# Opening a projection phase with two weight slabs at once

## The chip, the cores and the metric

One core of a Trainium2 chip runs the kernel. The metric is the device time of one execution in microseconds; the profile is of one such execution. Engines are named as the profile does: PE is TensorE (matmuls), DVE VectorE, ACT ScalarE, POOL GpSimd, SP the engine that issues most DMAs.

## The reference

One inference step of a two-layer encoder for 544 tokens (512 of a prompt, 32 of a sample), model width 1024, all in fp32:

```
layer 0: h = rmsnorm(x); u,v,z,xbc,dt = h @ W_in
         x += concat(gmlp(u, v), rmsnorm(ssd(xbc, dt) * silu(z))) @ W_out
layer 1: h = rmsnorm(x); q,k,v,g = h @ W_in      (8 retention heads)
         x += (silu(g) * head_norm(retention(q, k, v))) @ W_out
each:    h = rmsnorm(x); x += (silu(conv3(h @ W_gate)) * (h @ W_up)) @ W_down
         x += sigmoid(rmsnorm(x) @ W_pgate) * (p @ W_pproj)
end:     y = rmsnorm(x)
```

Here rmsnorm(x) is x times the reciprocal root of the mean of its squares over the 1024 features, times a gain per feature.

## The kernel before

**Layout.** Features lie on the 128 partitions and the 544 tokens along the free dimension, so x is eight tiles of 128x544. An operand of a projection is held twice, as `op_hi` (rounded to the matmul's format) and `op_lo` (the rest), eight tiles each. Weights come in slabs: one slab (128 x 1024) holds the eight 128x128 blocks that give one output tile. A slab is loaded to `w_raw` and split into `w_hi` by ACT (`split_high`, L340) and `w_lo` by POOL (`split_low`, L414). There are four slots (RING = 4), and slab s+4 is split when slab s has been multiplied.

**A slab on PE** (`slab`, matmul at L318). For each operand tile k it makes three passes (w_hi x op_hi, w_hi x op_lo, w_lo x op_hi), each in two halves of the tokens: 6 matmuls a tile, 48 a slab. It signals `tile_done` at the end. The output `proj` has room for two slabs; a slab waits until DVE has evicted the output of the one before the last (`tile_read`). Slabs are grouped in phases, run in the order written in `phase_table`.

**Norms.** The scale 1/rms of a token is applied at the eviction of the outputs, not to the operand, so a phase can start before its norm is known. While the phase ahead ends, each finished tile of x goes through: ACT writes op_hi (`act_operand`, L376) and the square (L384), DVE writes op_lo (`dve_operand`, L389), POOL adds the square to `ssq` (`pool_square`, L405). After the last tile PE sums `ssq` over partitions with two matmuls against ones (`mean_square`, L329 and L330), ACT takes the root (`act_root`, L363 and L364), DVE the reciprocal (`dve_rstd`, L369). Only then can the first slab of the phase be evicted (`scaled`, L1393 and L1396, reads `rstd`).

**The openings.** Four phases have operands that carry a norm so computed: `outb` (norm n_yb), `gu00` (n_ffn0), `heads_a` (n_mix1) and `gu10` (n_ffn1). In each, PE runs slab 0, waiting for every tile's op_lo by the argument `ready`, then `mean_square`, then slab 1, slab 2 and so on. Phases gate0 and gate1 also carry a norm, but their `mean_square` stands between pp and gate.

**Order on the other engines.** Each engine's order is written out by hand. ACT and POOL run `phase(name, job)`: for each slab n first the split of slab n+4 (`split_ahead`, which waits for `tile_done` of slab n; `low_ahead`), then the job. In the gate phases ACT's job is the sigmoid of the evicted tile, and then op_hi and the square of the updated x; POOL's job adds the square. DVE between them multiplies the gate by `p_proj` (L1753) and adds to x (L1755). In gate1 the slabs from the fifth on have no slab s+4, so nothing is split there.

In a gate-up phase (gu) even slabs are the gate branch: DVE evicts, copies two columns of conv state (L1697), makes three taps (L1707, L1709), ACT makes SiLU, POOL multiplies by `rstd` (L604), and only then DVE evicts the odd slab (L1717, L1718).

Of the kernel before, what the change touches and what calls it, by code (L numbers as in the profile page):

```python
# [115 lines left out]
def build(nc, A, O):  # L116
# [27 lines left out]
    with ctx:  # L144
# [197 lines left out]
        def split_ahead(act, ph, n):  # L342

            s = n + ph.s0
            if not n.k and s.c + RING >= NSLABS:
                return
            g = (n * ph.m) + (ph.g0 + ph.m)
            act.wait_ge(tile_done, g.v)
            split_high(act, s + RING)
# [67 lines left out]
        def low_ahead(pool, ph, n):  # L417
            s = n + (ph.s0 + RING)
            if n.k or s.c < NSLABS:
                split_low(pool, s)  # L420
# [6 lines left out]
        HID = (1, 0)  # L427
        U_FIRST = 4
        WARM = 8
        V_SCALED = {1: (0, 1, 2), 3: (3, 4, 5), 4: (6, 7)}  # L430
        SSD_PIECES = ((1, 1, 5, 2, 2),) * NC + ((1, 1, 5, 2, 3),)
        SSD_MIXED = ((), (2,), (3,), (5,), (6,))
# [98 lines left out]
        @block.gpsimd  # L531
        def _(pool):
            sub, mul = ALU.subtract, ALU.mult

            def phase(name, job=None, per=4):
                def one(n):
                    low_ahead(pool, PH[name], n)
                    if job:
                        job(n)
                each_ahead(pool, PH[name], one, per)  # L540

            pool_squares(pool, "n_in", None)
            for n in range(RING):
                split_low(pool, At(n))
            pool.wait_ge(sem("wdt_hi"), 1)
            nc.gpsimd.tensor_tensor(w_dt_lo[:, :], w_dt[:, :], w_dt_hi[:, :], sub).then_inc(sem("wdt_lo"), 1)
            phase("v")

            phase("u")
            phase("xbc")  # L550
            low_ahead(pool, PH["outa"], At(0))

            def chunk(p, rows):

                pool.wait_ge(sem("x_copied"), 3 * p + 3)
                if p:
                    pool.wait_ge(sem("y_turned"), 2 * p)
                c = NC if p == 0 else p - 1
                three = lambda b, n: b[0:rows, 0:n * SP_].rearrange("p (h q) -> p h q", h=n)
                nc.gpsimd.tensor_tensor(three(y_tok, SH), three(x_tok, SH),  # L560
                                        head_rows[0:rows, 2 * SH:3 * SH].unsqueeze(2).broadcast_to([rows, SH, SP_]),
                                        mul).then_inc(sem("y_skip"), 1)
                pool.wait_ge(sem("xs_done"), p + 1)
                if p:
                    pool.wait_ge(sem("st_mm"), 2 * p)
                nc.gpsimd.tensor_tensor(three(xsd, SH), three(xs, SH),
                                        dte[0:rows, c * SH:(c + 1) * SH].unsqueeze(2).broadcast_to([rows, SH, SP_]),
                                        mul).then_inc(sem("xsd_done"), 1)

            for p in range(NC + 1):  # L570
                chunk(p, TS if p == 0 else CH)
                for n in SSD_MIXED[p] + SSD_END[p]:
                    low_ahead(pool, PH["outa"], At(n))
            pool_squares(pool, "n_yb", "n_in")
            phase("z", lambda n: pool_square(pool, "n_yb", n))
            pool_squares(pool, "n_ffn0", "n_yb")
            phase("outb", lambda n: pool_square(pool, "n_ffn0", n))

            for layer in range(2):
                if layer:  # L580
                    def head(name, h, h0):

                        for r_ in range(6):
                            n = (h + -h0) * 6 + r_
                            low_ahead(pool, PH[name], n)
                            if r_ < 2:
                                pool.wait_ge(sem("r_swap"), (h * 2 + (r_ + 1)).v)
                                nc.gpsimd.tensor_tensor(rot_sw, rot_sw, (sin_k, sin_q)[r_], mul)\
                                    .then_inc(sem("r_sin"), 1)
                    heads(pool, head, lambda: phase("ret_a"))  # L590
                    pool_squares(pool, "n_ffn1", "n_mix1")
                    phase("ret_b", lambda n: pool_square(pool, "n_ffn1", n))
                off = 0
                for part_, nt in enumerate(FFN_PARTS):
                    gu = PH[f"gu{layer}{part_}"]

                    def gated(n, off=off, gu=gu):
                        if n.mod(2):
                            return
                        t = n.div(2) + (off + layer * FT)  # L600
                        q = n.div(2).mod(2)
                        pool.wait_ge(sem("f_silu"), (t + 1).v)
                        pool.wait_ge(tile_read, (n + (gu.g0 - 2)).v)
                        nc.gpsimd.tensor_tensor(fsgr[:, q * T:(q + 1) * T], fsg[:, q * T:(q + 1) * T], rstd[:, :],  # L604
                                                mul).then_inc(sem("f_scaled"), 1)
                    phase(f"gu{layer}{part_}", gated)
                    if part_ == 2:
                        pool_squares(pool, PLE[layer], LAYER[layer])
                        phase(f"down{layer}2", lambda n: pool_square(pool, PLE[layer], n))
                    else:  # L610
                        phase(f"down{layer}{part_}")
                    off += nt
                phase(f"pp{layer}")
                nxt = ("n_mix1", "n_out")[layer]
                pool_squares(pool, nxt, PLE[layer])
                phase(f"gate{layer}", lambda n: pool_square(pool, nxt, n))


        @block.scalar
        def _(act):  # L620
# [3 lines left out]
                    ins.then_inc(sem(signal), 1)  # L624
                return ins

            def phase(name, job=None, per=4, peel=0):
                def one(n):
                    split_ahead(act, PH[name], n)
                    if job:  # L630
                        job(n)
                each_ahead(act, PH[name], one, per, peel)

            def updated(name, g0):
# [156 lines left out]
            for layer in range(2):  # L791
# [115 lines left out]
                def gate_job(n):  # L907
# [6 lines left out]
                        act_operand(act, nxt, n, part(x, n, 0, T))  # L914
                    else:
                        act_square(act, nxt, n, part(x, n, 0, T))
                phase(f"gate{layer}", gate_job)
                act_root(act, nxt)
            act.wait_ge(sem("ret_stored"), 1 + 32 * RH)

# [2 lines left out]
        def _(pe):  # L923
            def mm(out, w, o, start=True, stop=True):
                return nc.tensor.matmul(out, w, o, start=start, stop=stop)  # L925

            def phase(name, ops, ready=None, per=4, hook=None, k0=0, start=0):

                ph = PH[name]

                def one(n):
                    slab(pe, ph, n, ops, ready, k0)
                    if hook and not n.k and n.c == 0:
                        hook()
                each(pe, ph.slabs, one, per, peel=4 if hook else 0, least=2)

            def norm(name):
                def hook():
                    mean_square(pe, name)
                return hook  # L940

            def v_turn(g):
                q = g % 2
# [196 lines left out]
                chunk(p, TS if p == 0 else CH)  # L1140
            assert done[0] == KD * KD
            phase("z", 0)
            phase("outb", 1, (nsem("lo"), ncount("n_yb", "lo", 1)), hook=norm("n_yb"))

            for layer in range(2):
                if layer:
# [64 lines left out]
                    def head(name, h, h0):  # L1211
                        n = (h + -h0) * 6
                        first = not h.k and h.c == 0
                        last = not h.k and h.c == RH - 1
                        for r_ in range(6):
                            if not first and r_ < 5:
                                turns[r_](h + -1)
                            if last and r_ == 5:
                                turn1(h)
                                slab(pe, PH[name], n + r_, 1, ks=range(0, 4))  # L1220
                                turn2(h)
                                slab(pe, PH[name], n + r_, 1, ks=range(4, 8))
                                continue
                            slab(pe, PH[name], n + r_, 1, (nsem("lo"), ncount("n_mix1", "lo", 1)) if first and r_ == 0 else None)
                            if first and r_ == 0:
                                mean_square(pe, "n_mix1")

                    ready_b = (sem("r_mlo"), 9)

# [16 lines left out]
                off = 0  # L1246
                for part_, nt in enumerate(FFN_PARTS):
                    if part_ == 0:
                        phase(f"gu{layer}0", 1 - HID[layer], (nsem("lo"), ncount(LAYER[layer], "lo", 1)), hook=norm(LAYER[layer]))
                    else:  # L1250
                        phase(f"gu{layer}{part_}", 1 - HID[layer])
                    phase(f"down{layer}{part_}", HID[layer], (sem("f_lo"), layer * FT + off + 1))
                    off += nt
# [619 lines left out]
```

## Time and profile before

| | |
|---|---|
| median of 3 runs | 1858.17 us (1857.85 to 1858.92) |
| the profiled execution | 1858.24 us |
| its span, first to last instruction | 1856.5 us |
| PE busy | 1816.7 us (98%) |
| DVE, ACT, POOL busy | 955.9, 622.5, 847.5 us |
| mean granted clock of PE | 0.991 |

The span is 1.7 us shorter than the time of the same execution. All times in rows are of this span. A line number such as L318 is a line of the kernel; a number in square brackets at the end of a timeline row is how long the engine was idle before it, and who ended that.

### The profile page before, as it was taken

The page shows a single profiled execution, that of the slowest core. Times are in us where ns is not written, and L with a number is a line of the kernel's source. Part 1 is how long each engine was busy: PE and PEld are TensorE (multiplying, and loading weights), DVE is VectorE, ACT ScalarE, POOL GpSimd, SP SyncE. Part 2 cuts the span into 40 slices and gives each one's busy share as a digit, 9 for nine tenths or more (in the row PEclk, how much of TensorE's full clock was granted, in tenths as well). Part 3 has the DMA queues.
Part 4 walks back from the last instruction along what each step waited for, and adds up shares of the span by engine and source line. Part 5 has one row for each costly group of instructions (what it writes and reads, how often), then busy time and mean ns, then how long its engine had stood idle before and what let it go on. Part 6 is the DMA issues. An engine that isn't in the chain of part 4 may idle for free.

```text
span 1856.5 us, 34451 instructions
## 1 busy us (share of the span) xinstructions
PE 1816.7 (98%) x14145; PEld 1768.9 (95%) x14145; DVE 955.9 (51%) x1547; ACT 622.5 (34%) x896; POOL 847.5 (46%) x415
## 2 busy tenths in 40 slices
PE   8999999999999999999899999999999999999996
PEld 7999988999999999999899999999899999999995
DVE  6456777565533542556644441344555415515554
ACT  5334423343221222244433332233334313212342
POOL 4333423466544544565533334333365545544662
PEclk9999999999999999999999999999999999999998
DMA  6222201222342232223222222222122222222221
GB/s 231 79 73 69 80 23 35 74 86 80 114 138 89 81 103 90 74 79 98 80 77 77 77 76 80 88 77 78 54 91 82 89 90 90 91 92 82 66 93 48
DMA packets 49475, 156.80 MB, mean 84 GB/s; under 512 B 5984, under 2 KB 10208, under 8 KB 49376
## 3 DMA queue, kind: packets, MB, share of 16 engines
q1 hardware_dynamic: 43776, 147.67, 24.4%
q10 hardware_dynamic: 5600, 7.74, 1.3%
q8 instruction: 71, 1.16, 0.3%
q14 instruction: 28, 0.23, 0.0%
HBM read 149.75 MB, written 5.63 MB: 84 GB/s over the span
## 4 chain that ended last, share of the span: by engine, by line
PE 90%; DVE 6%; ACT 2%; issue 1%; POOL 0%; DMA 0%; DVEq 0%; POOLq 0%; ACTq 0%
PE proj L318 81%; PE Q L925 6%; DVE arena L1753 1%; ACT arena L622 1%; DVE op_lo L389 1%; DVE arena L1616 0%; DVE arena L1606 0%; ACT op_hi L376 0%; PE Q L1202 0%; DVE rstd L369 0%; DVE x L1755 0%; DVE ssq L1426 0%; PE proj L925 0%; DVE arena L1393 0%; PE Q L329 0%
## 5 line engine op out<-in xcount | busy, mean ns | idle before, releaser
L414 POOL TENSOR_TENSOR w_lo<-w_raw,w_hi 128x1024 fp32r<-128x1024 f32 (+2 forms) x276 | 652.3, 2364 | 760.0 <-ACT w_hi L340 759.7
L318 PE MATMUL proj<-op_hi,w_hi 128*128 128x256 f32 (+1 forms) x4272 | 895.6, 291 | 9.5 <-DVE op_lo L389 5.7
L318 PE MATMUL proj<-op_hi,w_lo 128*128 128x256 f32 (+1 forms) x4272 | 884.6, 288 | 0.0
L318 PE MATMUL proj<-op_lo,w_hi 128*128 128x256 f32 (+1 forms) x4272 | 877.8, 287 | 0.0
L318 PEld LDWEIGHTS proj<-op_hi,w_hi 128*128 128x128 f32 x4272 | 683.5, 189 | 22.6 <-issue 12.3
L318 PEld LDWEIGHTS proj<-op_lo,w_hi 128*128 128x128 f32 x4272 | 686.3, 189 | 0.0
L318 PEld LDWEIGHTS proj<-op_hi,w_lo 128*128 128x128 f32 x4272 | 682.0, 188 | 0.0
L340 ACT ACTIVATE w_hi<-w_raw 128x1024 fp32r<-128x1024 f32 (+2 forms) x276 | 284.8, 1032 | 651.0 <-PE proj L318 650.0
L1393 DVE TENSOR_TENSOR arena<-proj,rstd 128x512 f32<-128x512 f32 (+1 forms) x143 | 98.7, 690 | 220.9 <-PE proj L318 195.4
L1400 DVE TENSOR_TENSOR x<-proj,x 128x512 f32<-128x512 f32 x72 | 49.7, 690 | 223.2 <-PE proj L318 223.2
L622 ACT ACTIVATE arena<-arena 128x32 f32<-128x32 f32 (+5 forms) x217 | 106.0, 514 | 54.6 <-DVE arena L1606 33.2
L604 POOL TENSOR_TENSOR arena<-arena,rstd 128x544 f32<-128x544 f32 x44 | 60.0, 1363 | 140.6 <-ACT arena L622 140.6
L405 POOL TENSOR_TENSOR ssq<-ssq,sq 128x544 f32<-128x544 f32 x56 | 90.3, 1613 | 67.7 <-ACT sq L384 67.7
L925 PE MATMUL Q<-arena 128*128 128x256 f32 (+9 forms) x524 | 104.7, 344 | 1.3 <-DVE arena L1616 0.8
L1709 DVE SCALAR_TENSOR_TENSOR arena<-arena,vec 128x546 f32<-128x546 f32 x88 | 96.4, 1095 | 12.4 <-DVE arena L1709 0.3
L925 PEld LDWEIGHTS Q<-arena 128*128 128x128 f32 (+3 forms) x524 | 71.9, 178 | 25.6 <-issue 16.2
L1717 DVE TENSOR_TENSOR arena<-proj,arena 128x512 f32<-128x512 f32 x44 | 30.4, 692 | 120.0 <-POOL arena L604 120.0
L389 DVE SCALAR_TENSOR_TENSOR op_lo<-x,vec,op_hi 128x544 fp32r<-128x544 f32 x48 | 72.1, 1514 | 37.0 <-ACT op_hi L376 33.5
L1707 DVE TENSOR_SCALAR arena<-arena,vec 128x546 f32<-128x546 f32 x44 | 78.2, 1777 | 8.3 <-DVE arena L1697 8.3
L622 ACT ACTIVATE ffn_tail<-arena 128x4 f32 (+1 forms) x44 | 9.1, 206 | 200.0 <-DVE arena L1709 200.0
L1720 DVE TENSOR_TENSOR op_lo<-arena,op_hi 128x544 f32 (+1 forms) x44 | 47.5, 1080 | 40.3 <-ACT op_hi L622 40.3
L622 ACT ACTIVATE op_hi<-arena 128x544 f32 (+2 forms) x46 | 31.0, 678 | 67.5 <-DVE arena L1718 67.5
(171 smaller groups left out, 1040.2 us busy)
## 6 DMA issues: line engine op xcount, KB each, us to landing
w_raw<-in_w_gu SPq DMA_DIRECT2D x88, 512.0 KB, 3.4
w_raw<-in_w_down SPq DMA_DIRECT2D x32, 512.0 KB, 3.4
w_raw<-in_w_heads_a SPq DMA_DIRECT2D x30, 512.0 KB, 3.4
w_raw<-in_w_heads_b SPq DMA_DIRECT2D x18, 512.0 KB, 3.4
w_raw<-in_w_gate SPq DMA_DIRECT2D x16, 512.0 KB, 3.4
w_raw<-in_w_xbc SPq DMA_DIRECT2D x12, 512.0 KB, 3.3
w_raw<-in_w_down SPq DMA_DIRECT2D x16, 384.0 KB, 3.0
w_raw<-in_w_v SPq DMA_DIRECT2D x8, 512.0 KB, 8.2
```

The lines of the kernel that those rows point to most:

```text
L318: last = nc.tensor.matmul(proj[:, 2 * g.mod(2) + half, 0:size], w[:, lo:lo + P], o[:, at:at + size], start=(k == 0 and j == 0), stop=(k == ...
L340: nc.scalar.activation(w_hi[:, c:c + width], w_raw[:, c:c + width], ACT.Copy).then_inc(w_hi_done, 1)
L389: nc.vector.scalar_tensor_tensor(out=part(op_lo[ops], n, 0, T), in0=src, scalar=col(gain, n), in1=part(op_hi[ops], n, 0, T), op0=ALU.mult, ...
L405: nc.gpsimd.tensor_tensor(ssq[:, :], ssq[:, :], sq[:, q * T:(q + 1) * T], ALU.add)\
L414: nc.gpsimd.tensor_tensor(w_lo[:, c:c + width], w_raw[:, c:c + width], w_hi[:, c:c + width], ALU.subtract).then_inc(w_lo_done, 1)
L604: nc.gpsimd.tensor_tensor(fsgr[:, q * T:(q + 1) * T], fsg[:, q * T:(q + 1) * T], rstd[:, :], mul).then_inc(sem("f_scaled"), 1)
L622: ins = nc.scalar.activation(dst, src, f, **kw)
L925: return nc.tensor.matmul(out, w, o, start=start, stop=stop)
L1393: a = tt(two(dst(0, TP)), out_prompt(g, rows), two(by[0:rows, f_at:f_at + TP]), mul)
L1400: tt(two(part(x, n, 0, TP)), out_prompt(g), two(part(x, n, 0, TP)), add)
L1707: ins = nc.vector.tensor_scalar(acc, src, w, col(f"fb{layer}", t + -layer * FT), mul, add)
L1709: ins = stt(out=acc, in0=src, scalar=w, in1=acc, op0=mul, op1=add)
```

## The change

At the four openings PE runs two slabs together (`paired`): tiles 0 to 6 of slab 0, tiles 0 to 4 of slab 1 (PAIR_MS = 5), the two matmuls of the mean square, tiles 5 and 6 of slab 1, the last tile of slab 0, the last tile of slab 1. Slab 2 and the rest follow as before. In the gate phases ACT and POOL handle the last tile (n = 7) before they split a slab, where before they split first.

```
--- before.py
+++ after.py
@@ -427,6 +427,7 @@
         HID = (1, 0)
         U_FIRST = 4
         WARM = 8
+        PAIR_MS = 5
         V_SCALED = {1: (0, 1, 2), 3: (3, 4, 5), 4: (6, 7)}
         SSD_PIECES = ((1, 1, 5, 2, 2),) * NC + ((1, 1, 5, 2, 3),)
         SSD_MIXED = ((), (2,), (3,), (5,), (6,))
@@ -532,11 +533,15 @@
         def _(pool):
             sub, mul = ALU.subtract, ALU.mult
 
-            def phase(name, job=None, per=4):
+            def phase(name, job=None, per=4, late=None):
                 def one(n):
-                    low_ahead(pool, PH[name], n)
+                    last = not n.k and n.c == late
+                    if not last:
+                        low_ahead(pool, PH[name], n)
                     if job:
                         job(n)
+                    if last:
+                        low_ahead(pool, PH[name], n)
                 each_ahead(pool, PH[name], one, per)
 
             pool_squares(pool, "n_in", None)
@@ -613,7 +618,7 @@
                 phase(f"pp{layer}")
                 nxt = ("n_mix1", "n_out")[layer]
                 pool_squares(pool, nxt, PLE[layer])
-                phase(f"gate{layer}", lambda n: pool_square(pool, nxt, n))
+                phase(f"gate{layer}", lambda n: pool_square(pool, nxt, n), late=KD - 1)
 
 
         @block.scalar
@@ -624,11 +629,15 @@
                     ins.then_inc(sem(signal), 1)
                 return ins
 
-            def phase(name, job=None, per=4, peel=0):
+            def phase(name, job=None, per=4, peel=0, late=None):
                 def one(n):
-                    split_ahead(act, PH[name], n)
+                    last = not n.k and n.c == late
+                    if not last:
+                        split_ahead(act, PH[name], n)
                     if job:
                         job(n)
+                    if last:
+                        split_ahead(act, PH[name], n)
                 each_ahead(act, PH[name], one, per, peel)
 
             def updated(name, g0):
@@ -914,7 +923,7 @@
                         act_operand(act, nxt, n, part(x, n, 0, T))
                     else:
                         act_square(act, nxt, n, part(x, n, 0, T))
-                phase(f"gate{layer}", gate_job)
+                phase(f"gate{layer}", gate_job, late=KD - 1)
                 act_root(act, nxt)
             act.wait_ge(sem("ret_stored"), 1 + 32 * RH)
 
@@ -924,20 +933,28 @@
             def mm(out, w, o, start=True, stop=True):
                 return nc.tensor.matmul(out, w, o, start=start, stop=stop)
 
-            def phase(name, ops, ready=None, per=4, hook=None, k0=0, start=0):
+            def phase(name, ops, ready=None, per=4, k0=0):
 
                 ph = PH[name]
-
-                def one(n):
-                    slab(pe, ph, n, ops, ready, k0)
-                    if hook and not n.k and n.c == 0:
-                        hook()
-                each(pe, ph.slabs, one, per, peel=4 if hook else 0, least=2)
-
-            def norm(name):
-                def hook():
-                    mean_square(pe, name)
-                return hook
+                each(pe, ph.slabs, lambda n: slab(pe, ph, n, ops, ready, k0), per, least=2)
+
+            def paired(name, ops, norm):
+
+                ph = PH[name]
+                ready = (nsem("lo"), ncount(norm, "lo", 1))
+                last = ph.kt - 1
+                slab(pe, ph, At(0), ops, ready, ks=range(0, last))
+                slab(pe, ph, At(1), ops, ks=range(0, PAIR_MS))
+                mean_square(pe, norm)
+                slab(pe, ph, At(1), ops, ks=range(PAIR_MS, last))
+                slab(pe, ph, At(0), ops, ready, ks=range(last, last + 1))
+                slab(pe, ph, At(1), ops, ks=range(last, last + 1))
+
+            def normed(name, ops, norm):
+
+                paired(name, ops, norm)
+                ph = PH[name]
+                each(pe, ph.slabs, lambda n: slab(pe, ph, n, ops) if n.k or n.c >= 2 else None, 4, peel=4, least=2)
 
             def v_turn(g):
                 q = g % 2
@@ -1140,7 +1157,7 @@
                 chunk(p, TS if p == 0 else CH)
             assert done[0] == KD * KD
             phase("z", 0)
-            phase("outb", 1, (nsem("lo"), ncount("n_yb", "lo", 1)), hook=norm("n_yb"))
+            normed("outb", 1, "n_yb")
 
             for layer in range(2):
                 if layer:
@@ -1221,9 +1238,10 @@
                                 turn2(h)
                                 slab(pe, PH[name], n + r_, 1, ks=range(4, 8))
                                 continue
-                            slab(pe, PH[name], n + r_, 1, (nsem("lo"), ncount("n_mix1", "lo", 1)) if first and r_ == 0 else None)
                             if first and r_ == 0:
-                                mean_square(pe, "n_mix1")
+                                paired(name, 1, "n_mix1")
+                            elif not (first and r_ == 1):
+                                slab(pe, PH[name], n + r_, 1)
 
                     ready_b = (sem("r_mlo"), 9)
 
@@ -1246,7 +1264,7 @@
                 off = 0
                 for part_, nt in enumerate(FFN_PARTS):
                     if part_ == 0:
-                        phase(f"gu{layer}0", 1 - HID[layer], (nsem("lo"), ncount(LAYER[layer], "lo", 1)), hook=norm(LAYER[layer]))
+                        normed(f"gu{layer}0", 1 - HID[layer], LAYER[layer])
                     else:
                         phase(f"gu{layer}{part_}", 1 - HID[layer])
                     phase(f"down{layer}{part_}", HID[layer], (sem("f_lo"), layer * FT + off + 1))
```

## Rows read from the trace of the kernel before

**Rows 1.** The page, part 1: busy time, share of the span, instructions.

```profile
PE 1816.7 (98%) x14145; PEld 1768.9 (95%) x14145; DVE 955.9 (51%) x1547; ACT 622.5 (34%) x896; POOL 847.5 (46%) x415
```

**Rows 2.** TensorE's waits, whole span: total us, times, longest us.

```profile
PE proj L318 <- DVE op_lo L389: 5.7, 2, 5.2
...
PE Q L329 <- POOL ssq L405: 5.4, 2, 5.2
```

**Rows 3.** The chain of waits: start us, us, what; one slab.

```profile
54.34 5.99 PE proj L318 x48
```

**Rows 4.** Timeline, opening of gu00: start us, us, instruction [idle before].

```profile
437.61 1.85 POOL L405 TENSOR_TENSOR ssq<-ssq,sq 128x544 f32<-128x544 f32 x1
...
439.62 0.59 PE L329 MATMUL Q<-ssq,ones 128*128 128x256 f32 x2
...
445.85 0.18 DVE L1396 TENSOR_TENSOR arena<-proj,rstd 128x32 f32<-128x32 f32 x1
...
453.10 0.49 PE L318 MATMUL proj<-op_hi,w_hi 128*128 128x256 f32 x2 [0.43 <-issue]
```

**Rows 5.** Timeline, opening of outb.

```profile
383.73 0.69 DVE L1393 TENSOR_TENSOR arena<-proj,rstd 128x512 f32<-128x512 f32 x1 [0.27 <-PE proj L318]
...
390.71 0.48 PE L329 MATMUL Q<-ssq,ones 128*128 128x256 f32 x1 [0.18 <-POOL ssq L405]
...
397.03 0.18 DVE L1396 TENSOR_TENSOR arena<-proj,rstd 128x32 f32<-128x32 f32 x1
```

**Rows 6.** Timeline, opening of gu10.

```profile
1381.63 0.59 PE L329 MATMUL Q<-ssq,ones 128*128 128x256 f32 x2
...
1383.63 1.28 ACT L340 ACT_TABLE_LOAD   x1
...
1386.06 2.39 POOL L414 TENSOR_TENSOR w_lo<-w_raw,w_hi 128x1024 fp32r<-128x1024 f32 x1 [4.87 <-ACT w_hi L340]
...
1388.30 0.18 DVE L1697 COPY arena<-ffn_state 128x2 f32 x1
...
1396.09 0.49 PE L318 MATMUL proj<-op_hi,w_hi 128*128 128x256 f32 x2 [1.39 <-issue]
...
1397.81 2.45 POOL L414 TENSOR_TENSOR w_lo<-w_raw,w_hi 128x1024 fp32r<-128x1024 f32 x1 [0.40 <-ACT w_hi L340]
...
1398.61 1.67 DVE L1697 COPY arena<-ffn_state 128x2 f32 x1
```

**Rows 7.** Timeline, last tile of gate0 and opening of heads_a.

```profile
898.02 2.35 POOL L414 TENSOR_TENSOR w_lo<-w_raw,w_hi 128x1024 fp32r<-128x1024 f32 x1
...
898.26 2.70 DVE L1753 TENSOR_TENSOR arena<-arena 128x544 f32<-128x544 f32 x1 [0.73 <-ACT arena L622]
...
903.12 1.40 POOL L405 TENSOR_TENSOR ssq<-ssq,sq 128x544 f32<-128x544 f32 x1 [2.75 <-ACT sq L384]
...
903.37 0.82 PE L318 MATMUL proj<-op_hi,w_hi 128*128 128x256 f32 x2 [5.18 <-DVE op_lo L389]
...
904.90 0.63 PE L329 MATMUL Q<-ssq,ones 128*128 128x256 f32 x1
...
912.12 0.18 DVE L1396 TENSOR_TENSOR arena<-proj,rstd 128x32 f32<-128x32 f32 x1
...
924.44 0.68 DVE L1393 TENSOR_TENSOR arena<-proj,rstd 128x512 f32<-128x512 f32 x1
```

**Rows 8.** Timeline, gate1: the fourth and the fifth tile's multiply.

```profile
1813.54 2.47 DVE L1753 TENSOR_TENSOR arena<-arena 128x544 f32<-128x544 f32 x1 [0.85 <-ACT arena L622]
...
1819.40 0.72 DVE L1753 TENSOR_TENSOR arena<-arena 128x544 f32<-128x544 f32 x1 [0.72 <-ACT arena L622]
```

**Rows 9.** Timeline, TensorE in the SSD part.

```profile
225.67 0.43 PE L925 MATMUL Q<-tri,arena 32*32 32x32 f32 x8 [1.45 <-DVE arena L1606]
```

**Rows 10.** Two stretches: us, busy time of each engine, PEclk, DMA share, GB/s.

```profile
225.00:235.00 10.00, 9.13 (x65) 8.54 (x66) 5.70 (x20) 1.24 (x4) 3.65 (x2) 0.66 0.14 51
...
903.00:909.00 6.00, 5.63 (x21) 5.17 (x22) 1.47 (x2) 3.23 (x6) 1.47 (x2) 0.50 0.05 19
```

## Prediction

> **What bounds the kernel now.** I read the page first: TensorE is busy 98% of the span [rows 1], and the chain of waits is a string of whole slabs of projection matmuls, each of 48 matmuls in 6.0 us [rows 3]. So 0.125 us a matmul, 0.75 us for one operand tile (three passes by two halves), 5.25 us for seven tiles. TensorE sets the time nearly everywhere; what it waits for at a phase's opening is lost one to one, and nothing else the change does can win. TensorE's list of waits comes next: for the low half of an operand tile 5.7 us in all, of which one wait of 5.2; for the sum of squares 5.4 us, of which 5.2 in one [rows 2]. That one is the final norm's at 1841 us, which no edited order reaches. So at the four edited openings (outb, gu00, heads_a, gu10) nearly all that can be removed is one wait, at heads_a. The timelines of the four openings then show what is late in each [rows 4 to 7].
>
> **Two limits at an opening.** Call t the start of slab 0. Before, the mean square is issued at t+6.0, or later where the last tile's low half or the last square is late. After it come the root on ScalarE, the reciprocal on VectorE and the eviction of slab 0, without which slab 2 has no PSUM bank. This chain takes 6.4 us from mean square to the end of the eviction at gu00 (439.62 to 446.03) [rows 4] and 6.5 at outb (390.71 to 397.21) [rows 5]. TensorE covers it with the two mean square matmuls (about 0.7 us) and slab 1 (6.0), 6.7 in all: the chain just fits, by 0.2 to 0.3 us.
>
> After, the mean square stands behind 7+5 tiles: t+9.0. Only 3+1 tiles are left behind it (tiles 5 and 6 of slab 1, and the last tile of both), 3.0+0.7 us of cover for the same 6.4 to 6.5 us. Slab 2 must wait 2.7 to 2.8 us. In general slab 2 starts at the later of t+9.0 and the last square, plus 6.5; before it started at the later of t+6.0 and that square (or the last tile), plus 6.7. Pairing therefore loses wherever the square was there before t+9, and wins at most 0.2 us where it was not. That is the heart of the forecast: the change takes cover from a chain that had just enough, to cover waits that are, except at heads_a, below 0.6 us.
>
> **outb.** t is about 383.5 (VectorE's eviction of z's last tile starts at 383.73, some 0.2 us behind it). Mean square before at 390.71 after waits on the low half and the squares, so 7.2 behind t [rows 5]; slab 2 at 390.7+6.7 = 397.5. After: 383.5+9.0+6.5 = 399.0. Loss 1.5 us. Later slabs have DVE room, so nothing is regained.
>
> **gu00.** The last square is there at 437.61+1.85 = 439.46, 0.16 us ahead of the mean square at 439.62: no wait [rows 4]. Here slab 3 counts. It needs the eviction of slab 1, which stands behind the three taps, SiLU, and GpSimd's multiply; it starts 13.5 us behind the mean square, having waited 0.43 [rows 4]. With the mean square 3.0 later, all of this is 3.0 later. One more thing moves: the first weight split waits for tile_done of slab 0, now at t+12 and not t+6, so GpSimd's w_lo (2.4 us) falls onto VectorE's copy at L1697. That copy takes 0.18 us alone and 1.67 when it meets a w_lo, ending with it [rows 6]. At gu00 w_lo would end at about 449.3 and the copy want 449.0: 0.2 to 0.3 more. Loss 3.2.
>
> **gu10.** Same shape: mean square at 1381.63, exactly on time; slab 3 at 1396.09 behind a wait of 1.39 [rows 6]. Loss 3.0, plus the split: ScalarE has a table load of 1.28 us in front of the first w_hi [rows 6], and if it waits for tile_done first, w_lo runs until 1392.6 while the copy wants 1391.3, so 1.2 more. I take 4.2; the bounds are 3.0 and 4.3.
>
> **gate0 to heads_a.** Two edits meet. The late order: now the last tile's multiply on VectorE takes 2.70 us beside GpSimd's w_lo of 2.35 [rows 7]. In gate1 the fourth tile's takes 2.47, the fifth's, whose slab has no split behind it, 0.72 [rows 8]. Putting w_lo behind the square therefore takes 2.0 us off the last tile: low half at 901.3 and not 903.3, last square at 902.5 and not 904.5. The moved w_hi (1.05) and w_lo (2.4) then end by 905; slab 3, which needs them, starts after 915, so they cost nothing; without that cover they would cost their 3.4 us. Ahead of the root, ScalarE must fit w_hi and its table load behind the last square: done at about 903.4, root wanted at 903.7. No DMA is issued at a moved place; SP's loads hang on splits that lie far ahead.
> The Trainium skill (SBUF — State Buffer, Who interferes with whom) has the rule: a VectorE instruction with two SBUF inputs and a GpSimd instruction that reads SBUF exclude each other for their whole length. By it the saving is the whole remaining w_lo; the rows agree at 2.0 us.
>
> The pair: t is 892.8 (seven tiles ended at 903.37-5.18 = 898.19) [rows 7]. Slab 1's five tiles fill 898.0 to 901.8, its bank having been freed at 897.5. The mean square waits for the square until 902.6 (before 904.90), at full clock; eviction of slab 0 ends at 909.0, before at 912.3 [rows 7]. The next slabs are bound by VectorE's rotary chain behind that eviction: the third eviction starts at 924.44 and ends 925.2, which before was just ahead of slab 4's own turn at 925.5. All this moves by 3.3 to 3.4. Gain 3.4. Of this the late order alone gives nearly everything: it would put the mean square at 902.6 too. With slab 1 behind it slab 2 would start at 909.3, so pairing adds next to nothing even here.
>
> In gate1 the last slab has no split to be moved, so that edit is nothing there. The unrolled instruction count of TensorE is unchanged.
>
> **Sum.** +1.5 +3.2 -3.4 +4.2 = +5.5 us on the profiled execution's 1858.24, which is 0.07 us above the median of the runs: 1863.7.
>
> **The clock.** What these rows don't price is the granted clock behind the new idle stretches. Before: after 5.18 us idle it was 0.50 (1.2 GHz) over 903 to 909; in the SSD part a gap of 1.45 us among small matmuls was followed by 0.66 over 225 to 235 [rows 7, 9, 10]; the 1.39 us gap at gu10 left the next matmuls at full pace, as the 0.49 us of its first pair shows against 0.82 after the long gap [rows 6, 7]. The new gaps, five of them (outb 2.8, gu00 2.7, heads_a 2.7, gu10 3.0 and 2.9), lie between. From both sides: none falls, 0; all fall. One fall costs about 3.1 us of matmuls: the pair pace goes from 0.25 to 0.46 us as at 903, over six to seven us. Part is hidden where a later slab waits anyway: 3.1 at outb, 1.8 at gu00, 2.1 at heads_a, 0.2 and 3.1 at gu10, together 10.3. The new gaps have full matmuls on both sides, as the harmless one had, but are twice its length; I take one to two falls, 3.3 us.
> The Trainium skill (TensorE: Matmul & The Clock Gate, Part 1) says that the gate's watch is not started by the kernel, so the place of a change shifts between runs. No row here shows that; by it the result would spread by some us from run to run.
>
> Forecast: 1858.2+5.5+3.3 = **1867.0 us**, slower by 0.5%.
>
> **Rivals.**
> 1. Loss without any fall of the clock: 1863.7. For it: 1.39 us left it alone. Chance 0.27.
> 2. The clock falls at every new gap: 1858.2+5.5+10.3 = 1874. Chance 0.13.
> 3. Faster: slab 2 is not held by the eviction chain, because root and reciprocal turn out to be covered. Then outb, gu00 and gu10 lose nothing and heads_a gains up to 4.5 us (slab 2 at 909.0, before at 913.5, its clock no longer halved): 1853.7. It decides if the chain from mean square to eviction is under 3.8 us; the reciprocal alone takes 3.55 in all eight places. Against it, all rows. Chance 0.05.
> 4. No change beyond 0.2%: gu10's split brings nothing (3.0), outb loses 1, heads_a gains the full 4.5, no clock falls: +2 to +3, 1861. Chance 0.10.
> 5. The forecast, one or two falls: 0.45.
>
> A measurement of this kernel tells from no change about 0.2%, 3.7 us: 1854.5 to 1861.9. Slower 0.85, same 0.10, faster 0.05. The range reaches from just above the border, where rival 4 ends, to just under every fall: 1861.5 to 1873.
>
> **What the profile would show.** Right: TensorE's waits on VectorE's eviction of about 2.7 us at outb's and gu00's third slab, at heads_a's and gu10's too, and near 1 (gu00) and 2 to 3 us (gu10) at the fourth; mean square at 9.0 us behind slab 0's start; the 5.18 us wait gone and one below 1 us for the square in its place; the last L1753 of gate0 at 0.72; half-clock stretches behind one or two of the openings. Wrong: no wait at slab 2 anywhere, or the clock full throughout with other gains; or the last multiply of gate0 still at 2.7, which would put heads_a's gain at 1.3 and the total 2 us higher.

## The result and the profile after

The changed kernel takes 1866.51 us (median of 6 runs, 1864.05 to 1866.79) against 1858.20 for the kernel before: 8.3 us more, ratio 1.004 with a 95% interval of 1.0029 to 1.0051. It is slower. The profiled execution took 1866.49 us with a span of 1864.7 us, 8.2 us longer than before.

Line numbers have moved: L1396, L1697, L1718 and L1753 of before are L1414, L1715, L1736 and L1771 of after. TensorE's list of waits after (total us, times, longest us), which answers to [rows 2]:

```profile
PE proj L318 <- DVE arena L1414: 10.3, 4, 2.8
...
PE Q L329 <- POOL ssq L405: 5.9, 2, 5.2
...
PE proj L318 <- DVE arena L1736: 3.9, 2, 2.8
```

The wait of 5.2 us for the low half has gone from the list. Four waits for the eviction of slab 0 have come, 10.3 us, and two for that of slab 1, 3.9 us. The 5.2 us for the final norm's squares stand as before. The timelines of the four openings after answer to [rows 4 to 7]. At outb, in order of time (start us, us, instruction, idle before):

```profile
393.14 0.59 PE L329 MATMUL Q<-ssq,ones 128*128 128x256 f32 x2
...
399.35 0.18 DVE L1414 TENSOR_TENSOR arena<-proj,rstd 128x32 f32<-128x32 f32 x1
...
399.68 0.49 PE L318 MATMUL proj<-op_hi,w_hi 128*128 128x256 f32 x2 [2.45 <-DVE arena L1414]
```

The eviction of slab 0 ends 6.4 us behind the mean square, and slab 2 starts 6.5 us behind it after an idle stretch of 2.45 us. At gu00:

```profile
444.65 0.59 PE L329 MATMUL Q<-ssq,ones 128*128 128x256 f32 x2
...
449.16 2.35 POOL L414 TENSOR_TENSOR w_lo<-w_raw,w_hi 128x1024 fp32r<-128x1024 f32 x1 [7.66 <-ACT w_hi L340]
...
450.97 0.56 DVE L1715 COPY arena<-ffn_state 128x2 f32<-128x2 f32 x1
...
451.20 0.49 PE L318 MATMUL proj<-op_hi,w_hi 128*128 128x256 f32 x2 [2.47 <-DVE arena L1414]
...
458.56 0.49 PE L318 MATMUL proj<-op_hi,w_hi 128*128 128x256 f32 x2 [1.14 <-DVE arena L1736]
```

Slab 2 waits 2.47 us and slab 3 another 1.14. The first w_lo ends at 451.51; the copy at L1715 that starts at 450.97 ends with it, 0.56 us for 0.16. At heads_a:

```profile
897.21 2.75 DVE L1771 TENSOR_TENSOR arena<-arena 128x544 f32<-128x544 f32 x1 [0.72 <-ACT arena L627]
...
903.74 0.73 DVE L1771 TENSOR_TENSOR arena<-arena 128x544 f32<-128x544 f32 x1 [0.72 <-ACT arena L627]
...
908.00 2.38 POOL L414 TENSOR_TENSOR w_lo<-w_raw,w_hi 128x1024 fp32r<-128x1024 f32 x1
...
908.09 0.70 PE L329 MATMUL Q<-ssq,ones 128*128 128x256 f32 x2 [0.69 <-POOL ssq L405]
...
914.49 0.18 DVE L1414 TENSOR_TENSOR arena<-proj,rstd 128x32 f32<-128x32 f32 x1
...
914.82 0.80 PE L318 MATMUL proj<-op_hi,w_hi 128*128 128x256 f32 x2 [2.53 <-DVE arena L1414]
```

The seventh multiply of gate0, beside a w_lo, takes 2.75 us, the eighth, with the w_lo put behind the square, 0.73. The mean square waits 0.69 us for the square, and slab 2 waits 2.53 us. At gu10:

```profile
1387.07 0.59 PE L329 MATMUL Q<-ssq,ones 128*128 128x256 f32 x2
...
1390.51 1.28 ACT L340 ACT_TABLE_LOAD   x1 [1.47 <-PE proj L318]
...
1392.94 2.38 POOL L414 TENSOR_TENSOR w_lo<-w_raw,w_hi 128x1024 fp32r<-128x1024 f32 x1 [9.31 <-ACT w_hi L340]
...
1393.74 1.60 DVE L1715 COPY arena<-ffn_state 128x2 f32 x1
...
1393.97 0.49 PE L318 MATMUL proj<-op_hi,w_hi 128*128 128x256 f32 x2 [2.82 <-DVE arena L1414]
...
1402.97 0.80 PE L318 MATMUL proj<-op_hi,w_hi 128*128 128x256 f32 x2 [2.75 <-DVE arena L1736]
```

The table load of 1.28 us now comes after the wait for tile_done, so the w_lo runs from 1392.94 to 1395.32 and the copy takes 1.60 us. Slab 2 waits 2.82 us, slab 3 another 2.75. The granted clock behind the last two openings (columns as in [rows 10]):

```profile
914.00:918.00 4.00, 3.18 (x15) 3.21 (x16) 2.06 (x4) 2.37 (x3) 2.96 (x3) 0.57 0.38 130
...
918.00:924.00 6.00, 6.00 (x51) 6.00 (x50) 3.82 (x5) 2.38 (x3) 3.28 (x3) 1.00 0.29 88
...
1402.00:1406.00 4.00, 3.03 (x14) 3.06 (x15) 3.02 (x6) 1.60 (x2) 3.60 (x2) 0.57 0.12 23
...
1406.00:1412.00 6.00, 6.00 (x51) 6.00 (x50) 3.23 (x4) 1.80 (x4) 2.28 (x2) 1.00 0.44 162
```

The clock, 0.57 in the mean of 914 to 918 and of 1402 to 1406, is half (1.2 GHz) for most of these stretches and full again behind them. The first pair of matmuls takes 0.80 us at both places, against 0.49 at outb and gu00, where the clock stayed full.

**Where the 8.2 us are.** A slab 0 now starts 9.0 us ahead of its mean square, before 6.0. So t was 383.5 and is 384.1 at outb; 433.6 and 435.6 at gu00; 1375.6 and 1378.1 at gu10. Slab 3 of gu00 went from 453.10 to 458.56, slab 3 of gu10 from 1396.09 to 1402.97. This gives:

| stretch | measured | forecast |
|---|---|---|
| ahead of all edited code | +0.6 | 0 |
| outb | +1.4 | +1.5 |
| gu00, up to slab 3 | +3.4 | +3.2 |
| heads_a | -3.0 | -3.4, clock apart |
| gu10, up to slab 3 | +4.4 | +4.2 |
| behind slab 3 of gu10 | +1.3 | clock |

The first row is not the change's. Nothing ahead of outb was edited, but in the SSD part the granted clock was 0.50 in the mean over 225 to 235 in this execution and 0.66 in the profiled one of before [rows 10]. VectorE's step that waits for TensorE there (L1634 of before, L1652 of after) started at 237.74 before and at 238.40 after, behind idle times of 5.88 and 6.93 us:

```profile
225.00:235.00 10.00, 9.77 (x60) 9.16 (x61) 5.25 (x18) 1.23 (x4) 3.20 (x2) 0.50 0.10 41
...
237.74 1.44 DVE L1634 TENSOR_TENSOR arena<-Q,arena 32x512 f32<-32x512 f32 x2 [5.88 <-PE Q L925]
...
238.40 1.44 DVE L1652 TENSOR_TENSOR arena<-Q,arena 32x512 f32<-32x512 f32 x2 [6.93 <-PE Q L934]
```

### The profile page after: what moved, and what is told of

Read it like the earlier page. It is cut to its first block, busy times and chain, and to the rows that moved or that the text cites. A ratio compares the mean times of both kernels' runs of the same rounds, so it can differ in the third digit from the quotient of the medians.

```text
span 1864.7 us, 34436 instructions
## 1 busy us (share of the span) xinstructions
PE 1817.9 (97%) x14145; PEld 1770.0 (95%) x14145; DVE 955.9 (51%) x1547; ACT 622.8 (33%) x896; POOL 848.3 (45%) x415
## 4 chain that ended last, share of the span: by engine, by line
PE 88%; DVE 7%; ACT 2%; issue 2%; POOL 0%; DMA 0%; DVEq 0%; POOLq 0%; ACTq 0%
PE proj L318 79%; PE Q L934 6%; DVE rstd L369 1%; DVE arena L1771 1%; ACT arena L627 1%; DVE op_lo L389 1%; DVE arena L1634 0%; DVE ssq L1444 0%; DVE arena L1624 0%; DVE arena L1411 0%; PE Q L1219 0%; ACT op_hi L376 0%; DVE x L1773 0%; DVE arena L1727 0%; PE proj L934 0%
## 5 line engine op out<-in xcount | busy, mean ns | idle before, releaser
L318 PE MATMUL proj<-op_hi,w_hi 128*128 128x256 f32 (+1 forms) x4272 | 896.6, 291 | 16.3 <-DVE arena L1414 10.3
L934 PE MATMUL Q<-arena 128*128 128x256 f32 (+9 forms) x524 | 104.7, 345 | 1.3 <-DVE arena L1634 0.8
L934 PEld LDWEIGHTS Q<-arena 128*128 128x128 f32 (+3 forms) x524 | 71.9, 178 | 25.6 <-issue 16.2
```

Of the source, the lines that this page charges most:

```text
L318: last = nc.tensor.matmul(proj[:, 2 * g.mod(2) + half, 0:size], w[:, lo:lo + P], o[:, at:at + size], start=(k == 0 and j == 0), stop=(k == ...
```

## Experiments

The chips' runs of the kernel before had medians of 1858.05 to 1858.26 us beside these.

**1. The late order alone** (`late_only`): the kernel before with the edit of the gate phases on ScalarE (its line is shown) and the same one on GpSimd.

```
-                phase(f"gate{layer}", gate_job)
+                phase(f"gate{layer}", gate_job, late=KD - 1)
```

> The kernel before with the late order alone, no pairs. Theory 1 (the chain from mean square to the first eviction decides each opening, and GpSimd's split beside the last multiply held heads_a): last multiply of gate0 0.72 us, mean square of heads_a about 2.3 us earlier, slab 2 at the same place as with the pair; the first wait for the low half shrinks from 5.2 to 3.2 us; total 1854.8 us (3.4 below before). Rival (the pair is what removes the 5.2 us wait, the late order only its 2.0 us): 1856.2.

1855.54 us (11 runs), ratio 0.9986 (0.9977 to 0.9995): 2.7 us below before, not 3.4. Its timeline at the end of gate0:

```profile
899.20 0.73 DVE L1761 TENSOR_TENSOR arena<-arena 128x544 f32<-128x544 f32 x1 [0.73 <-ACT arena L626]
...
902.10 1.40 POOL L405 TENSOR_TENSOR ssq<-ssq,sq 128x544 f32<-128x544 f32 x1 [3.10 <-ACT sq L384]
...
902.35 0.83 PE L318 MATMUL proj<-op_hi,w_hi 128*128 128x256 f32 x2 [3.22 <-DVE op_lo L389]
```

The multiply is at 0.73 us and the wait for the low half at 3.22, both as expected. This profiled execution is one of the two of eleven above 1857 us (1857.31). It lies 1.2 us behind the one of experiment 9 already ahead of outb, with a clock of 0.52 over 225 to 235, so its rows do not account for the median. What is missing from the 3.4 us at heads_a is the clock: behind the wait of 3.2 us it falls to half. Here the first pair takes 0.83 us, as behind the 5.18 us wait. In experiment 9, whose profiled execution took 1855.58 us, the first pair is still at full pace, and the clock is 0.57 over 902 to 906:

```profile
901.20 0.52 PE L318 MATMUL proj<-op_hi,w_hi 128*128 128x256 f32 x2 [3.24 <-DVE op_lo L389]
...
902.00:906.00 4.00, 3.81 (x14) 3.13 (x13) 0.48 (x1) 1.55 (x5) 2.66 (x2) 0.57 0.08 15
```

From the reciprocal of gu00 to that of gu10 (L369) the stretch is 942.07 us before and 939.69 in experiment 9, a gain of 2.4. With the clock kept full it is 938.74, a gain of 3.3, in experiment 12 (with the pair and filling matmuls at heads_a; its other edits lie outside this stretch).

**2. The pairs alone** (`pair_only`): the changed kernel without `late`.

> The changed kernel without the late order. Theory 1: outb, gu00 and gu10 lose as in the changed kernel; at heads_a the square is there 2.0 us later, a wait of about 2.8 us stands before its mean square, and that opening gains 1.0 to 1.3 in place of 3.0: 1868.3 us. Rival (the late order does nothing of its own, the pair hides the last tile anyway): 1866.5.

1868.08 us (5 runs), ratio 1.0054 (1.0040 to 1.0068). The multiply is back at 2.73 us, and the mean square waits 2.66 us for the square:

```profile
902.76 2.73 DVE L1771 TENSOR_TENSOR arena<-arena 128x544 f32<-128x544 f32 x1 [0.73 <-ACT arena L627]
...
907.67 1.38 POOL L405 TENSOR_TENSOR ssq<-ssq,sq 128x544 f32<-128x544 f32 x1 [2.75 <-ACT sq L384]
...
909.10 0.76 PE L329 MATMUL Q<-ssq,ones 128*128 128x256 f32 x1 [2.66 <-POOL ssq L405]
```

**3. The pair at heads_a alone, with the late order** (`pair_heads`).

```
 def normed(name, ops, norm):
-    paired(name, ops, norm)
     ...
+    slab(pe, ph, At(0), ops, ready)
+    mean_square(pe, norm)
     ...
```

> Pair at heads_a alone, late order kept, the other three openings as before the change. Theory 1: the three waits of 2.5 to 2.8 us at outb, gu00 and gu10 vanish, heads_a as in the changed kernel: 1854.8 us, within 0.5 of the late order alone. Rival (the pair earns its part at heads_a): at least 1 us below the late order alone.

1855.55 us (11 runs), the same as the late order alone to 0.01 us. The first three experiments together: the late order brings 2.7 us without the pairs and takes 1.6 us off them with them (1868.08 to 1866.51); the pair at heads_a brings nothing beside it; the other three pairs cost 1866.51 - 1855.55 = 11.0 us.

**4. The mean square early, the pairs kept** (`ms_early`).

```
-    paired(name, ops, norm)
+    paired(name, ops, norm, 1)
```

The new last argument of `paired` is the number of tiles of slab 1 ahead of the mean square, 5 where it isn't given.

> The changed kernel with the mean square after one tile of slab 1 (t+6.0) in place of five at outb, gu00 and gu10; heads_a keeps five. The pairs, the late tile_done and the later weight splits stay. Theory 1 (place of the mean square): slab 2 waits no more than 0.5 us, and only the split that falls on VectorE's taps costs, about 1 us at gu00 and 1.5 at gu10: 1857 to 1858.5 us. Rival (the later tile_done and the later splits cost, not the mean square): stays at 1864 to 1866.5.

1863.09 us (10 runs, 1860.64 to 1865.82), ratio 1.0025 (1.0015 to 1.0034). Neither number. Slab 2's wait is gone (0.23 us), but slab 3's grew. Its gu00:

```profile
440.70 0.60 PE L329 MATMUL Q<-ssq,ones 128*128 128x256 f32 x2
...
448.21 2.59 POOL L414 TENSOR_TENSOR w_lo<-w_raw,w_hi 128x1024 fp32r<-128x1024 f32 x1 [7.66 <-ACT w_hi L340]
...
448.58 3.64 DVE L1727 SCALAR_TENSOR_TENSOR arena<-arena,vec 128x546 f32<-128x546 f32 x2
...
456.98 0.80 PE L318 MATMUL proj<-op_hi,w_hi 128*128 128x256 f32 x2 [2.74 <-DVE arena L1736]
```

The first weight split starts only when slab 0 is done, at t+12, and with the mean square early again it falls on the taps: two taps take 3.64 us for 1.61, the second ending 1.4 us behind the w_lo. Slab 3 waits 2.74 us at gu00 and 3.28 at gu10. I had priced this at 1 to 1.5 us; it is 2.3 and 1.9 more than before's waits of 0.43 and 1.39. Behind the wait at gu00 the clock is 0.50 over 457 to 460, which comes on top.

**5. GpSimd's first split behind its multiply** (`ms_order`): experiment 4, and in gu00 and gu10 GpSimd's w_lo of slab 4 behind the multiply by rstd.

```
-                    phase(f"gu{layer}{part_}", gated)
+                    phase(f"gu{layer}{part_}", gated, late=None if part_ else 0, peel=0 if part_ else 4)
```

> The kernel with the early mean square (after one tile of slab 1 at three openings), and at gu00 and gu10 GpSimd's first w_lo moved behind its multiply by rstd. The pairs and the late tile_done stay. Theory 1b (what was left in the early kernel is that w_lo meeting the second tap): the taps' pair at gu00 back from 3.64 to 1.6 us, slab 3 waits 1 us at gu00 and 1.5 to 2 at gu10 in place of 2.75 and 3.28: 1856.5 us. Rival (late tile_done costs by itself, whatever w_lo meets): 1860 or more.

1857.84 us (11 runs, 1856.25 to 1858.45), ratio 0.9997 (0.9988 to 1.0006). The taps are at 1.61 us and slab 3 waits 0.67 us at gu00, 1.27 at gu10:

```profile
449.15 1.61 DVE L1727 SCALAR_TENSOR_TENSOR arena<-arena,vec 128x546 f32<-128x546 f32 x2
...
453.14 1.37 POOL L609 TENSOR_TENSOR arena<-arena,rstd 128x544 f32<-128x544 f32 x1 [12.03 <-ACT arena L627]
...
454.47 5.23 POOL L414 TENSOR_TENSOR w_lo<-w_raw,w_hi 128x1024 fp32r<-128x1024 f32 x2
...
455.48 0.49 PE L318 MATMUL proj<-op_hi,w_hi 128*128 128x256 f32 x2 [0.67 <-DVE arena L1736]
```

So of the 11.0 us that three pairs cost, and in this order of edits, 3.4 go with the mean square's place and 5.3 more with the w_lo that then met the taps. The 5.3 us are not a loss of the changed kernel, whose w_lo met only the copy (0.56 and 1.60 us): the early mean square brought that meeting about, so experiment 4 alone shows too little of what the mean square's place costs. They also hold the half clock at gu00, gone here. The edit on GpSimd was not run with the late mean square, so the two are told apart only in this order. The last 2.3 us over experiment 3 I place only in part. At outb the mean square now waits 1.01 us for the last square and slab 2 another 0.30, where in experiment 3 the waits are 0.56 and 0.18. Slab 2 waits 0.23 us at gu00 and gu10, and slab 3 of gu00 0.2 more than before. That is about 1.2 us; the rest is open.

**6. The idle stretches filled** (`fill`): the changed kernel, with matmuls whose output nobody reads.

```
+            def fill():
+                for _ in range(11):
+                    mm(Q[:, 0, 0:P], ones[:, :], ones[:, :])
```

> The changed kernel with 11 matmuls of ones (0.21 us each, 2.3 us, their output unused) put into each new idle stretch: ahead of slab 2 at the four openings and ahead of slab 3 at gu10. The waits keep their ends. Theory (the granted clock falls behind these stretches and that costs): no half clock at heads_a and gu10, 1863.5 to 1864.5 us, and the spread over runs smaller than 1864.05 to 1866.79. Rival (the clock costs nothing here, the waits are all): 1866.5.

1864.94 us (5 runs, 1863.89 to 1865.49), ratio 1.0037 (1.0024 to 1.0051), 1.6 us below the changed kernel. The stretches that were at 0.57:

```profile
914.00:918.00 4.00, 3.97 (x32) 4.00 (x32) 2.09 (x2) 2.30 (x3) 2.96 (x3) 1.00 0.39 131
...
1402.00:1406.00 4.00, 4.00 (x34) 4.00 (x33) 3.36 (x4) 1.31 (x2) 3.46 (x2) 1.00 0.42 127
```

Counted from each opening's mean square, slabs 2 and 3 of gu10 start where they did (6.90 and 15.90 us), the clock stays full, and 1.6 us come back. That is the clock's share of the 8.3 us. The runs of both kernels overlap by 1.4 us, so from the medians its size is good to about 1 us. The stretches of the two profiled executions (1863.89 and 1866.49 us) give nearly the same. From slab 3 of gu00 to slab 0 of gu10 the filled kernel takes 0.45 us less, and behind slab 3 of gu10 1.35 less, 1.8 together; the other 0.8 lies ahead of outb. The spread over runs is 1.6 us for 2.7.

**7. gu10 with its first four slabs written out** (`after_peel`): on ScalarE and VectorE.

```
-phase(gu.name, gate_up, peel=0 if off or layer else 4)
+phase(gu.name, gate_up, peel=0 if off else 4)
...
-each(dve, 2 * nt, gate_up, peel=0 if off or layer else 4)
+each(dve, 2 * nt, gate_up, peel=0 if off else 4)
```

> The changed kernel with the first four slabs of gu10 written out on ScalarE and VectorE (peel 4 in layer 1 too, as in layer 0). Theory: the table load of 1.28 us ahead of the first w_hi goes, w_lo ends earlier and the copy no longer meets it (1.60 to below 0.5 us), the 0.2 us steps of register work between the taps go: slab 3's wait 2.75 to about 1.1, 1864.5 us, or 1863.3 where the clock fall behind it goes too. Rival (the copy's delay is hidden): 1866.

1864.07 us (6 runs), ratio 1.0032 (1.0020 to 1.0044), 2.4 us below the changed kernel. No table load stands ahead of the first w_hi, and the copy takes 0.42 us:

```profile
1391.09 1.06 ACT L340 ACTIVATE w_hi<-w_raw 128x1024 fp32r<-128x1024 f32 x1 [1.39 <-PE proj L318]
...
1392.22 2.35 POOL L414 TENSOR_TENSOR w_lo<-w_raw,w_hi 128x1024 fp32r<-128x1024 f32 x1 [7.96 <-ACT w_hi L340]
...
1394.17 0.42 DVE L1715 COPY arena<-ffn_state 128x2 f32<-128x2 f32 x1
```

Slab 3's wait went from 2.75 to 0.99 us. The steps of 0.2 us between the taps went too, so the 2.4 us are not the table load's alone. In the profiled execution no half clock follows at heads_a or gu10 either, so part of the gain may be the clock's.

**8. Without pairs, late order in z too, and the four slabs written out** (`late_z_peel`): the kernel of experiment 1 with the edit of 7 and, on ScalarE and GpSimd, this one.

```
-            phase("z", z_job)
+            phase("z", z_job, late=KD - 1)
```

> No pairs: the kernel before with the late order in gate and in z, and peel 4 in layer 1. Theory: z's last multiply 2.47 to 0.72 us, the waits of 0.6 and 0.2 us at outb gone (about 1 us in all), slab 3's wait at gu10 1.39 to 0.4: 1853.6 us, 2 us below the late order alone. Rival (outb's waits are only moved to a later slab): 1854.6.

1853.94 us (11 runs), ratio 0.9978 (0.9969 to 0.9987). Both gains came: no wait of 0.3 us or more at outb, 0.57 at gu10's slab 3.

**9. The late order on GpSimd alone** (`late_pool`).

> The kernel before with the late order on GpSimd alone; ScalarE splits first as before. Theory (the whole gain is VectorE's multiply no longer held by w_lo): the same as the late order on both, 1855.5 us. Rival (ScalarE's w_hi of 1.05 us ahead of the sigmoid holds the last tile too): 1856.5.

1855.78 us (11 runs), ratio 0.9990 (0.9981 to 0.9999): the same as with ScalarE's part. The gain is the multiply freed from the w_lo; ScalarE's order is worth nothing that these runs can tell.

**10 and 11. The job ahead of the split for every tile**, in gate (`gate_first`) and in z too (`gate_z_first`): the kernel of experiment 8 with `late=-1`, taken as every tile.

> No pairs, late order in z, peel 4 in layer 1, and in the gate phases the job before the split for every tile, not the last alone. Theory (VectorE falls behind TensorE by 0.54 us a slab in gate0 because each multiply is held by w_lo, 2.75 for 0.72 us, and that lag is the rest of the wait at heads_a): multiplies of 0.7 to 1.5 us, slabs evicted within 0.3 us of their end, the wait at heads_a 3.2 us to below 0.5, 1851 us. Rival (w_lo now runs into the next multiply just as long): 1853.9, as the late order.

> The same with the job before the split for every tile of z too. Both theories: z keeps pace with TensorE already (6.0 us a slab), so its last tile gains nothing more: within 0.5 us of the kernel with gate alone.

1854.56 and 1854.60 us (11 runs each), ratio 0.9981 for both, 0.6 us above experiment 8 and not 3 below. My theory fell. VectorE's multiplies of gate0 in experiment 10, the first, the seventh and the eighth:

```profile
851.62 0.73 DVE L1761 TENSOR_TENSOR arena<-arena 128x544 f32<-128x544 f32 x1 [0.72 <-ACT arena L626]
...
888.80 2.75 DVE L1761 TENSOR_TENSOR arena<-arena 128x544 f32<-128x544 f32 x1 [0.73 <-ACT arena L626]
...
895.34 2.72 DVE L1761 TENSOR_TENSOR arena<-arena 128x544 f32<-128x544 f32 x1 [0.72 <-ACT arena L626]
```

and GpSimd beside the last:

```profile
893.72 1.43 POOL L405 TENSOR_TENSOR ssq<-ssq,sq 128x544 f32<-128x544 f32 x1 [2.75 <-ACT sq L384]
...
895.10 2.38 POOL L414 TENSOR_TENSOR w_lo<-w_raw,w_hi 128x1024 fp32r<-128x1024 f32 x1
```

The w_lo now starts as the square ends, and the next multiply comes 0.24 us behind it. The square hangs on the multiply, the w_lo on the square and the next multiply on the w_lo: the three lock at 6.54 us a tile (888.80 to 895.34). That is before's cadence too, with the split ahead of the job (891.72 to 898.26, [rows 7]):

```profile
891.72 2.75 DVE L1753 TENSOR_TENSOR arena<-arena 128x544 f32<-128x544 f32 x1 [0.72 <-ACT arena L622]
```

The new order starts the last multiply 1.8 us sooner than experiment 8 does (895.34 for 897.16) and then holds it 2.0 us longer (2.72 for 0.73). The wait for the last tile's low half is 3.70 us, 3.20 in experiment 8.

**12. Pair at heads_a and fill, on the kernel of experiment 8** (`heads_fill`).

> No pairs but at heads_a; late order in gate and z, peel 4 in layer 1, and the 11 matmuls of ones ahead of slab 2 of heads_a. Theory (the one gain left in the pair is that its idle stretches are short enough to be filled, so that the clock stays full, where the unpaired order has one wait of 3.2 us and a half clock behind it): no half clock at heads_a, 0.5 to 1 us below the late order with z and peel: 1853.2 us. Rival (VectorE's rotary chain bounds the next slabs whatever the clock): 1853.9.

1852.68 us (7 runs, 1852.32 to 1853.51), ratio 0.9970 (0.9959 to 0.9981), 1.3 us below experiment 8 and the fastest of all. The fill's matmuls (at L934, each of the 11 counted as two in the profile) stand between the end of the pair and the eviction that slab 2 waits for, and the clock is 1.00 over 906 to 912:

```profile
902.00 0.70 PE L329 MATMUL Q<-ssq,ones 128*128 128x256 f32 x2 [0.68 <-POOL ssq L405]
...
906.02 2.62 PE L934 MATMUL Q<-ones 128*128 128x128 f32 x22
...
908.40 0.18 DVE L1418 TENSOR_TENSOR arena<-proj,rstd 128x32 f32<-128x32 f32 x1
```

The intervals of the two ratios overlap, but from gu00's reciprocal to gu10's this kernel takes 938.74 us and experiment 8 takes 939.70, so 1.0 us of the gain stands where the edit is. Pair and fill were put in together here; that the pair without fill brings nothing is known from experiment 3 on the kernel with the late order alone. Whether matmuls of this kind in the one wait of 3.2 us, without the pair, would bring the same was not run.

## Why the prediction was right

It said 1867.0 us, and 1866.51 was measured, within the range of 1861.5 to 1873 and slower as forecast. By its steps:

- **The two limits at an opening** held as written. The chain from mean square to the end of slab 0's eviction took 6.4 us at outb after, 6.5 from rows of before, and slab 2 waited 2.45 to 2.82 us at all four openings for the 2.7 to 3.0 forecast. Putting the mean square back at t+6.0 took slab 2's wait down to 0.23 to 0.30 us (experiments 4 and 5).
- **outb, gu00, gu10** came to 1.4, 3.4 and 4.4 us for 1.5, 3.2 and 4.2. The copy that meets the w_lo was there at both places, with the table load behind the wait as the larger value at gu10 assumed; experiment 7 took the load and the steps between the taps away and got 2.4 us back.
- **gate0 to heads_a** came to 3.0 us for 3.4. The 2.0 us off the last multiply were exact (experiments 1, 2 and 9), and the pair adds nothing there (experiment 3). The missing part is a clock fall behind slab 2's wait: with the stretches filled (experiment 6) the clock stays full and the gain is 3.5. The working has t at 892.8 where its own rows give 892.9; the mean square waits for the square there, so nothing hangs on it.
- **The clock** was mis-sized. One to two falls were right, two in the profiled run, but they cost 1.3 us behind gu10 and 0.45 at heads_a, 1.6 to 1.8 us together by experiment 6, for the 3.3 of the sum. I had taken one fall at the length seen behind the 5.18 us wait; behind waits of 2.5 and 2.75 us the clock was back sooner. The sum without the clock was forecast at 5.5 us. By the stretches of the filled kernel's profiled execution it is 5.7 (1.4, 3.4 and 4.4, less 3.5); by the medians it is 6.7 (1864.94 less 1858.2). The profiled execution of after holds another 0.6 us, of the clock in the unedited SSD part, which the forecast had at nothing. The misses cancel to half a microsecond; that the total is nearer than its clock term is luck.
- **The rivals.** The faster case needed a chain under 3.8 us; it was 6.4. The case with no clock fall (1863.7) is nearest to the lowest of the six runs, 1864.05, and to the filled kernel's profiled execution, 1863.89.

## What to carry to other kernels

Work that is put in front of a step to cover a wait is taken from the work behind that step: count the cover on both sides before moving it. Here the mean square had 0.2 us to spare behind it and lost 3 us of cover, to hide waits that were below 0.6 us at three places of four. A wait at the end of a phase is better looked for in the engine that is late than covered on the engine that waits: one w_lo moved behind one square on GpSimd gave 2.4 us (experiment 9), and the pair at heads_a by itself added nothing.

## What the runs showed of the hardware

VectorE operations with two inputs in SBUF, and the small copy too, end with GpSimd's running w_lo or up to one duration of their own behind it: 0.73 us became 2.75, the copy's 0.16 became 1.60, two taps' 1.61 became 3.64. The Trainium skill (SBUF — State Buffer, Who interferes with whom) states such a lock for the shared pair of ports; these rows agree, at these three lines. It can lock three engines to a cadence of 6.54 us, and the cadence is the same with the split written ahead of the square (before) and behind it (experiment 10).

Idle stretches of 2.5 and 2.75 us between full matmuls were followed by half clock in the profiled run of after, while those of 2.45 and 2.47 at outb and gu00, as long, were not. The same stretch of the same code differs too: slab 2's wait at heads_a, 2.52 to 2.56 us, had half clock behind it in the profiled executions of after and of experiments 3 and 4, and none in those of experiments 5 and 7. Without a pair, the wait there (3.20 to 5.18 us) had half clock behind it in all six kernels profiled: before and experiments 1 and 8 to 11.
